# Attention of a hybrid encoder on one core: the values of the step behind placed ahead of the step's turns

## What is computed

```python
def block(args):                       # FoX, for 128 queries at a time
    logits = jnp.einsum('bqhd,bshd->bhqs', qb, k_all).astype(F32) * (hd ** -0.5)
    logits = logits + cqb.transpose(0, 2, 1)[..., None] - cum_t[:, :, None, :]
    logits = jnp.where(key_pos <= pb, logits, -jnp.inf)
    p = jax.nn.softmax(logits, axis=-1)
    return jnp.einsum('bhqs,bshd->bqhd', p.astype(v_all.dtype), v_all)
...
# DSA: the same softmax, over the keys that an indexer chose (top 128 of the prompt, top 72 for the sample)
```

## Time and profile before

| | |
|---|---|
| median of 3 runs | 1403.65 us (1403.59 to 1404.04) |
| the profiled execution | 1405.04 us |
| its span on the core | 1403.2 us |
| TensorE busy | 1376.6 us (98%) |
| VectorE, ScalarE, GpSimd busy | 584.3, 558.0, 592.9 us (42%, 40%, 42%) |
| granted TensorE clock | 0.999 |
| chain that ended last | TensorE 91%, VectorE 5%, ScalarE 2% |

### The profile page before, as it was taken

How to read it: one execution, slowest core, us unless ns; L and a number is a source line. 1 busy time by engine, 2 the same in 40 slices (tenths; PEclk the granted TensorE clock), 3 DMA queues, 4 the chain that set the end, 5 groups by cost and what they waited for, 6 DMA issues and landing times.

```text
span 1403.2 us, 27244 instructions
## 1 busy us (share of the span) xinstructions
PE 1376.6 (98%) x11012; PEld 1297.0 (92%) x11012; DVE 584.3 (42%) x1074; ACT 558.0 (40%) x903; POOL 592.9 (42%) x310
## 2 busy tenths in 40 slices
PE   9999999999999999999999999999999999999997
PEld 7878888999999999999988778778999999999997
DVE  5555566454321332122426956654633122211334
ACT  5546656344422333122464344344543223321223
POOL 5322222326443435334445376554344424443442
PEclk9999999999999999999999999999999999999999
DMA  5332122323342233322342422111233322332221
GB/s 162 99 91 63 52 65 64 111 76 91 90 119 76 75 90 105 90 61 70 89 102 61 91 92 76 42 32 31 76 90 90 106 73 77 90 107 74 82 68 64
DMA packets 206118, 114.39 MB, mean 82 GB/s; under 512 B 16548, under 2 KB 200792, under 8 KB 206040
## 3 DMA queue, kind: packets, MB, share of 16 engines
q1 hardware_dynamic: 200640, 109.39, 27.2%
q10 hardware_dynamic: 5400, 3.89, 0.9%
HBM read 107.30 MB, written 5.96 MB: 81 GB/s over the span
## 4 chain that ended last, share of the span: by engine, by line
PE 91%; DVE 5%; ACT 2%; issue 2%; ACTq 0%; DVEq 0%; POOL 0%; POOLq 0%
PE ps L1179 67%; PE ps L1438 3%; PE ps L1363 3%; DVE arena L2114 2%; PE ps L1392 2%; PE ps L1251 2%; PE ps L1408 2%; PE ps L1746 2%; PE ps L1378 2%; PE ps L1702 1%; PE ps L1714 1%; PE ps L1492 1%; PE ps L1234 1%; ACT arena L888 0%; PE ps L1738 0%
## 5 line engine op out<-in xcount | busy, mean ns | idle before, releaser
L618 POOL TENSOR_TENSOR w_lo<-w_raw,w_hi 128x1024 fp32r<-128x1024 f32 x197 | 489.6, 2489 | 694.8 <-ACT w_hi L700 694.8
L1179 PE MATMUL ps<-x_hi,w_hi 128*128 128x272 f32 x1792 | 373.2, 289 | 2.4 <-DVE arena L2091 2.0
L1179 PE MATMUL ps<-x_hi,w_lo 128*128 128x272 f32 x1792 | 370.9, 288 | 0.0
L1179 PE MATMUL ps<-x_lo,w_hi 128*128 128x272 f32 x1792 | 369.4, 288 | 0.0
L1179 PEld LDWEIGHTS ps<-x_hi,w_hi 128*128 128x128 f32 x1792 | 281.5, 188 | 6.8 <-issue 5.8
L1179 PEld LDWEIGHTS ps<-x_lo,w_hi 128*128 128x128 f32 x1792 | 281.6, 188 | 0.0
L1179 PEld LDWEIGHTS ps<-x_hi,w_lo 128*128 128x128 f32 x1792 | 279.7, 189 | 0.0
L700 ACT ACTIVATE w_hi<-w_raw 128x1024 fp32r<-128x1024 f32 x201 | 210.6, 1052 | 156.1 <-PE ps L1179 138.5
L1179 PE MATMUL ps<-o_hi,w_hi 128*128 128x272 f32 x864 | 179.2, 289 | 0.2 <-DVE xT L1955 0.2
L1179 PE MATMUL ps<-o_hi,w_lo 128*128 128x272 f32 x864 | 178.8, 288 | 0.0
L1179 PE MATMUL ps<-o_lo,w_hi 128*128 128x272 f32 x864 | 178.1, 288 | 0.0
(11 more groups left out here) (329 smaller groups left out, 1729.6 us busy)
## 6 DMA issues: line engine op xcount, KB each, us to landing
w_raw<-in_ffn_w_in SPq DMA_DIRECT2D x88, 512.0 KB, 3.8
w_raw<-in_ffn_w_out SPq DMA_DIRECT2D x32, 512.0 KB, 3.8
w_raw<-in_ab_w_in SPq DMA_DIRECT2D x28, 512.0 KB, 4.1
w_raw<-in_cd_w_in SPq DMA_DIRECT2D x13, 512.0 KB, 4.1
w_raw<-in_ffn_w_out SPq DMA_DIRECT2D x16, 384.0 KB, 3.4
w_raw<-in_ab_w_out SPq DMA_DIRECT2D x8, 512.0 KB, 4.1
arena<-in_x_prompt SPq DMA_DIRECT2D x4, 512.0 KB, 7.8
w_raw<-in_cd_w_in SPq DMA_DIRECT2D x8, 256.0 KB, 5.3
```

The source lines that it names most:

```text
L618: pool.tensor_tensor(wl[:, s, :], raw[:, s, :], wh[:, s, :].bitcast(F32), ALU.subtract).then_inc(lo_done, 1)
L1179: mm = pe.matmul(ps[0:M, b + h, 0:HALF], w[:, s, k * M:(k + 1) * M], xs[x][:, k, h * HALF:(h + 1) * HALF], start=(begin and k == ks[0] and ...
```

## The change

In TensorE's list, `values(s - 1)` moves from behind the masks and the second piece of step s to ahead of the step's turns. No other engine's list changes, and no instruction or semaphore count is added or taken away.

```diff
                             pe.wait_ge(at_c[e], 2 * NS - 2)
                         last_rows(1, range(3), end=False)
+                    if s >= 1:
+                        values(s - 1)
                     if s < 2 * NS:
                         turn(2 * s)
                         turn(2 * s + 1)
...
                         masks(2 * s + 5)
                     for n in pieces(s, True):
                         first_rows(n)
-                    if s >= 1:
-                        values(s - 1)
                     if s + 2 < 2 * NS:
                         logits(s + 2)
```

## The result

The changed kernel takes 1413.46 us (median of 6 runs, 1413.16 to 1415.31) against 1403.68 us for the kernel before (6 runs, 1403.56 to 1404.04): a ratio of 1.0065, 95% interval 1.0051 to 1.0079. That is 9.8 us more where 4.6 were forecast, and outside the range. The profiled execution took 1414.76 us with a span of 1412.9.

What follows compares the result with a forecast made beforehand. The prediction took TensorE, busy 98% of the span, to bound the kernel. Order +3.8, filled holes -4.7 and new waits +5.5 summed to +4.6 us, from 1403.65 to 1408.2 us, range 1402.9 to 1411.4 (8 in 10).

Steps and rivals of the forecast that it cites:

- What bounds the kernel, and that the copies' waits are a trap: Whole kernel: TensorE busy 98% of the span; the copies' long waits for values reach it only through VectorE's queue.
- What the order costs: TensorE's attention loop: changed neighbours of the moved values make the order dearer, +3.8 us.
- the first term: Masks right ahead of logits, waiting for the masks' semaphore: +0.12 us in 18 steps, +2.2 us.
- Values behind the half job: Values behind a half job or first_rows, where turns stood: +0.10 us in 16 steps, +1.6 us.
- that third term: Turns behind values, where logits stood: no difference taken, bounds -4.1 to +2.9 us over 24 steps.
- What the moved work fills: Holes ahead of turn_key and first_rows: values ahead of the turns runs inside them, -4.7 us.
- What is late next: Values of a new output waits for the previous output's low part on VectorE: +5.5 us.
- the five holes behind a `first_rows`: Steps 14, 17, 20, 23, 24: new holes of 0.84, 0.93, 0.93, 0.68, 0.83 us, +4.2 us.
- The hole of step 13: Ahead of values(12), with no block to cover it: hole of 2.2 us where it was 1.0, +1.2 us.
- free order: Rival: the order costs nothing and only holes count, 1404.4 us; chance 0.21 together with rival 4.
- A VectorE chain that starts earlier by itself: Rival, steps 13 to 24: each chain gains 0.85 us, offsetting all new waits; 1399.1 with free order; chance 0.08.
- Turns that cost a wait behind values: Rival: turns behind values cost +0.12 us in 24 steps, 2.9 us, giving 1411.1 us; chance 0.09.

Runs made afterwards that it cites:

- chosen steps: Kernel before, with values ahead of the turns only in steps 2, 15, 17, 19, 22 and masks ahead of the turns in 0 and 2: median 1401.87 us.
- the half with steps 1 to 12 alone: The change made in steps 1 to 12 only, against the kernel before: median 1407.87 us, ratio 1.0038.
- the change with the low part early: The change, plus VectorE making an output's low part ahead of the step's maxima: median 1406.51 us, ratio 1.0019 to the kernel before.
- turns behind the hole: Kernel before, but in step 13 TensorE waits for the low part ahead of the turns, values(12) unmoved: median 1408.51 us, ratio 1.0023.
- the moved wait: The change but in step 13, with the logits' fill_free wait moved ahead of the values: 1407.91 us, ratio 1.0025 to the kernel before.

## Why the prediction was wrong

Point by point, by its own steps:

- *What bounds the kernel, and that the copies' waits are a trap:* held. The 73 us of waits moved elsewhere and nothing came of it.
- *What the order costs,* +3.8 us: the order costs what it costs at the places that were named, but the first term was mis-sized. Masks to logits was taken as +0.12 us from a pair in step 0. But the logits of step 0 and of the prologue have one wait, and those from step 4 on two. The second costs 0.1 us more, where TensorE has nothing queued ahead of it: with it moved away the steps shorten by 0.1. From step 4 on it is +0.22. Values behind the half job is 0.07 to 0.1 and values to turns nothing, as taken; that third term was a choice inside bounds of -4.1 to +2.9 us, and came out well without a row behind it. Steps 1 to 12 cost 2.7 us, not 1.5.
- *What the moved work fills,* -4.7 us: held. The holes for `take_first_rows` and `turn_key` shrank from 5.1 to 0.8 us. The chosen steps gain 4.7 us too, but some 0.7 of it comes from the masks' place in two of them (0.20 in step 0, 7.25 - 6.71 = 0.54 in step 2).
- *What is late next,* +5.5 us: places and causes held, the sizes of the five holes behind a `first_rows` did not. They read 0.57, 0.64, 0.68, 0.44 and 0.54 us, 2.9 in all where 4.2 were forecast. The prediction's own rows give less for step 14 than it took: 903.47 + 0.57 + 0.15 - 901.82 - 1.71 = 0.66, not 0.84. The hole of step 13 was right (2.1). What failed is the step "it is 895.41 - 893.23 = 2.2: +1.2 us", which prices a hole at its length. Behind a hole of 2.1 us TensorE's clock fell, and step 13 cost 5.6 us; filling the hole with nothing of use takes 4.5 of them away. The rows of before showed the clock at its upper level through all its holes of the loop, up to 1.55 us, and the prediction went on from them without asking what a longer one does. It had no rival for this.
- *The sum:* 4.6 forecast, 4.4 more in step 13 and 1.2 more in steps 0 to 12 is 10.2; the runs measured 9.8, the steps 9.9. Steps 14 to 25 came out at 1.6 where 1.8 were worked out, by luck: shorter holes and a dearer order cancel.
- *The rivals:* free order is refuted by the half with steps 1 to 12 alone. A VectorE chain that starts earlier by itself and takes all the new waits away is refuted: 4.9 us of them are there, and they only go when the low part's place in VectorE's list is changed. In step 17 the maxima start 0.10 us behind the start of `first_rows` before (919.55 and 919.45) and 0.07 behind it after the change (927.50 and 927.43): 0.03 us earlier, where this rival had 0.85. Turns that cost a wait behind values are not seen (0.81 us either way).

Open: why the same hole brings the clock down in some executions and not in others, what part `values(12)` has in it, and why one of 1.0 us does so in most runs of the kernel of chosen steps and in none that we have a trace of before. Runs of before spread too on two of the three chips (up to 1410.6 and 1410.72 us), and those of the change with the low part early, with no such hole, up to 1412.39; what the clock did in them is not known.

## What to carry to other kernels

Price a hole in TensorE by what follows it as well: one of 2 us in front of thin matmuls cost 4.5 us more in clock than its own length. A semaphore wait that is long met isn't free everywhere: between two short blocks that depend on each other (masks and logits) it cost 0.1 us, ahead of a block of `values` nothing was seen of it; so put something between the two or wait earlier. And a change of order that helps five steps of 26 and hurts the rest should be made in the five.

## What the runs showed of the hardware that was not expected

The granted clock fell to its lower level behind holes of 2.1 us (in at least 4 of 10 runs with turns behind the hole, in all 11 with the 64-column matmuls of the sample, going by a mean clock of 0.994 to 0.996) and stayed there for up to 10 us while TensorE was busy for all but 0.2 of them: 0.61 and 0.55 on average over two stretches that make 12 us. Useless transposes in the hole kept it at 1.00 in step 13, in both traces. And in two kernels (the moved wait, the chosen steps) it fell 5.4 and 5.0 us behind a hole of 1.0 us, with TensorE busy in between, at the end of the thin matmuls of `values(12)`.
